# Three dummy matmuls, the first weights on ScalarE's queue, and a first half split one k tile at a time

## The chip, the cores and the metric

The kernel runs on one core of one Trainium2 chip. The metric is device time in microseconds, the median of the runs. Engines are TensorE (PE, with its weight loads as PEld), VectorE (DVE), ScalarE (ACT), GpSimd (POOL) and SyncE (SP). Transfers are issued by SP (queue q1), ScalarE (q10) and GpSimd (q0), and all queues are served by the same 16 DMA engines.

## What is computed

Two layers run one after the other on 256 tokens of width 2048, in float32. The first layer puts 16 meta tokens ahead (272 rows), normalizes, multiplies by a wide input matrix and runs two branches: attention over keys that an indexer selects, and a chunkwise gated recurrence. The second layer has a filter branch computed with Fourier transforms, grouped attention with rotary positions, and a gated feed-forward of width 5632. For the front of the program only this part of the reference matters:

```python
def rms_norm(x, gain):
    y = xf * lax.rsqrt(jnp.mean(xf * xf, axis=-1, keepdims=True) + EPS)
    return (y * gain.astype(jnp.float32)).astype(x.dtype)
...
h = rms_norm(x, norm_g)
proj = h @ w_in          # [272, 2048] @ [2048, 12368]
```

The kernel multiplies x by the gain ahead of the product and applies the reciprocal root to the product's rows, so the front needs the gain vector (norm_g) but not yet the root.

## The kernel before

**Products.** Every float32 product is made from rounded parts: an operand is split into a high part (rounded, written by ScalarE) and a low part (what is left, subtracted by VectorE), and a product is three matmuls, high by high, high by low and low by high (`product`, L2077 to L2080). The weights stream through in units of 512 rows by 512 columns (1 MB), four units to a chunk of 512 output columns. A unit lies in one of four slots of `raw` and is two halves of two k tiles (128 rows each). `split_half` on ScalarE (L758) writes `w_hi` for a half (128 x 1024), `split_half` on VectorE (L1280) writes `w_lo`, and TensorE's `chunk` waits for `split_lo` of the half, then issues its 12 matmuls (two k tiles, two blocks of 128 tokens, three matmuls). `w_hi` and `w_lo` have four slots each.

**Order.** There is no planner. Each engine's program is written out in order, and counting semaphores join them. A half has a number 8 q + h (chunk q, half h), and work beside the products is hung on these numbers (`branch_step`, `step`). In chunk 0 two more k tiles of x are turned behind each half, so that the operand is always four tiles ahead.

**The front, engine by engine.** SP issues the left half of x (two transfers, 512 KB each), then `raw[:, 0, 0:2]` (the first two k tiles of weights, semaphore `raw_first`, L580), `raw[:, 0, 2:4]` (L581), the second unit, the right half of x, two more units and a narrow block of weights. ScalarE issues the identity (64 KB), the gain vector into `stage_a` (8 KB; these two count `first_in`) and the meta tokens (128 KB). GpSimd waits for the left half of x and then issues thirty small constants.

TensorE waits for a cleared tile, runs `warm(4)` (four float32 matmuls on that tile, results unused; each is two passes in the profile), waits for `first_in`, turns the gain vector (L2210), waits until VectorE has copied it to `vec_a` (L1329), turns four k tiles of x (`turn_h`, L2204, which waits for x), runs `warm(2)` and enters chunk 0.

ScalarE evicts each turned tile as `h_hi`, scaled by the gain (`keep_h_hi`, L772), four of them, and then comes to the first `split_half`, which waits for `raw_first`. VectorE follows with `h_lo` (`keep_h_lo`, L1333), four of them, and then its `split_half`. In chunk 0 TensorE waits for `h_lo_kept` of both k tiles and for `split_lo` ahead of each half.

Of the kernel before, what the change touches and what calls it, by code (L numbers as in the profile page):

```python
# [15 lines left out]
F32 = mybir.dt.float32  # L16
F32R = mybir.dt.float32r
I32 = mybir.dt.int32
ALU = mybir.AluOpType
ACT = mybir.ActivationFunctionType  # L20
AX_X = mybir.AxisListType.X

P = 128
# [6 lines left out]
W = 512  # L30
# [32 lines left out]
def hybrid_layers(nc, a, out):  # L63

    ctx = ExitStack()
    with ctx:
# [6 lines left out]
        def place(name, shape, dt=F32):  # L73
            t = at(name, shape, dt, spot[0])
            spot[0] += -(-4 * int(np.prod(shape[1:])) // 32) * 32
            return t


        raw = place("raw", [P, 4, 4, W])
        w_hi = place("w_hi", [P, 4, 2, W], F32R)  # L80
        w_lo = place("w_lo", [P, 4, 2, W], F32R)
# [171 lines left out]
        def sem(name):  # L253
            return ctx.enter_context(nc.semaphore(name))
# [19 lines left out]
        meta_hi_kept = sem("meta_hi_kept")  # L274
        meta_lo_kept = sem("meta_lo_kept")
        raw_first = sem("raw_first")
        warm_ready = sem("warm_ready")
        raw_in = [sem(f"raw_in{s}") for s in range(4)]
        split_hi = sem("split_hi")
        split_lo = sem("split_lo")  # L280
# [16 lines left out]
        h_lo_kept = sem("h_lo_kept")  # L297
# [5 lines left out]
        rot_ready = sem("rot_ready")  # L303
        tables_ready = sem("tables_ready")
        rsq_ready = sem("rsq_ready")
        k_rstd = sem("k_rstd")
        k_scaled = sem("k_scaled")
        qk_turned = sem("qk_turned")
        qk_kept = sem("qk_kept")
# [75 lines left out]
        z_spec = sem("z_spec")  # L385
        y_spec = sem("y_spec")
        yh_prod = sem("yh_prod")
        yh_done = sem("yh_done")
        y_done = sem("y_done")
        y_biased = sem("y_biased")  # L390
        y_scaled = sem("y_scaled")
# [19 lines left out]
        w_in, w_branch, w_out = a["w_in"][0], a["w_branch"][0], a["w_out"][0]  # L411

        CHUNKS = [(C_QI, W, 0), (C_QI + W, W, 0), (C_QA, W, 0), (C_QA + W, W, 0),
                  (C_KA, W, 1), (C_VA, W, 1), (C_ZA, W, 0), (C_ZA + W, W, 0), (C_QB, W, 0), (C_QB + W, W, 0),
                  (C_ZB, W, 0), (C_ZB + W, W, 0), (C_FB, W, 1), (C_FB + W, W, 1), (C_IB, W, 1), (C_IB + W, W, 1)]
# [134 lines left out]
        def tile_rows(w, r0, rows, cols):  # L550
            return w[r0:r0 + rows, cols].rearrange("(k p) n -> p k n", p=P)
# [3 lines left out]
        def _(sp):  # L555
            def load_x(c):
                cols = slice(c * BW, (c + 1) * BW)
                for b in range(NT):
                    sp.dma_start(xt[:, b, cols], a["x"][0][b * P:(b + 1) * P, cols]).then_inc(x_in[c], 16)
# [17 lines left out]

            first_cols = slice(CHUNKS[0][0], CHUNKS[0][0] + W)
            load_x(0)
            sp.dma_start(raw[:, 0, 0:2, :], tile_rows(w_in, 0, 2 * P, first_cols)).then_inc(raw_first, 16)  # L580
            sp.dma_start(raw[:, 0, 2:4, :], tile_rows(w_in, 2 * P, 2 * P, first_cols)).then_inc(raw_in[0], 16)  # L581
            load_unit(0, 1, tile_rows(w_in, W, W, first_cols), first=True)
            load_x(1)
# [57 lines left out]
            for s in range(4):  # L641
                q = Q_DOWN + FKT // 4 - 1
# [93 lines left out]
        @block.scalar  # L736
        def _(act):
            act.dma_start(ident[:, :], a["c_ident"]).then_inc(first_in, 16)
            act.dma_start(stage_a[0:16, :], a["norm_g"].rearrange("o (k p) -> (o k) p", p=P)).then_inc(first_in, 16)
            act.dma_start(xm[:, :], a["meta_tokens"]).then_inc(meta_in, 16)  # L740

# [6 lines left out]

            def split_half(q, h, width=W, first=False):

                if first and h == 0:
                    act.wait_ge(raw_first, 16)
                elif h % 2 == 0 or (first and h == 1):
                    act.wait_ge(raw_in[h // 2], 16 * q + 16)
                if not (first and h < 4):

                    act.wait_ge(half_done, 8 * q + h - 3)
                act.activation(w_hi[:, h % 4, :, 0:width], raw[:, h // 2, 2 * (h % 2):2 * (h % 2) + 2, 0:width],  # L758
                               ACT.Copy).then_inc(split_hi, 1)

            n_roots = [0]

# [7 lines left out]
            def keep_h_hi(k):  # L770
                act.wait_ge(h_turned, k + 1)
                act.activation(h_hi[:, k, META:TM], ps[H_BANK[k]][:, 0:T], ACT.Copy, scale=vec_a[:, k:k + 1]  # L772
                               ).then_inc(h_hi_kept, 1)

            for k in range(4):
                keep_h_hi(k)

            def keep_turned_hi(g):
# [247 lines left out]
            def keep_y_hi(g):  # L1026

                for i, (at_slot, bank) in enumerate(YT):
                    if g == at_slot + 2:
                        act.wait_ge(y_turned, i + 1)  # L1030
                        keep_bank(y_hi[:, i // 4, 2 * (i % 4):2 * (i % 4) + 2, :].rearrange("p k t -> p (k t)"),
                                  bank).then_inc(y_hi_kept, 1)

            for n, (c0, width, m) in enumerate(CHUNKS):
                for h in range(8):
                    split_half(n, h, width, first=(n == 0))
                    if n == 1 and h == 3:
                        act.wait_ge(rs_ready, n_roots[0])
                        keep_chunk(0)
                    if h == 2 and n > 1 and n - 1 not in FM:  # L1040
                        keep_chunk(n - 1)
                    branch_step(8 * n + h)
                    keep_y_hi(8 * n + h)
# [224 lines left out]
        def _(dve):  # L1268
# [8 lines left out]
            def split_half(q, h, width=W):  # L1277

                dve.wait_ge(split_hi, 8 * q + h + 1)
                dve.tensor_tensor(w_lo[:, h % 4, :, 0:width], raw[:, h // 2, 2 * (h % 2):2 * (h % 2) + 2, 0:width],  # L1280
                                  w_hi[:, h % 4, :, 0:width].bitcast(F32), ALU.subtract).then_inc(split_lo, 1)
# [49 lines left out]
            def keep_h_lo(k):  # L1331
                dve.wait_ge(h_hi_kept, k + 1)
                dve.scalar_tensor_tensor(h_lo[:, k, META:TM], ps[H_BANK[k]][:, 0:T], vec_a[:, k:k + 1],  # L1333
                                         h_hi[:, k, META:TM].bitcast(F32), ALU.mult, ALU.subtract).then_inc(h_lo_kept, 1)

            for k in range(4):
                keep_h_lo(k)


# [377 lines left out]
            def keep_y_lo(g):  # L1717

                for i, (at_slot, bank) in enumerate(YT):
                    if g == at_slot + 2:  # L1720
                        dve.wait_ge(y_hi_kept, i + 1)
                        part = slice(2 * (i % 4), 2 * (i % 4) + 2)
                        dve.tensor_tensor(y_lo[:, i // 4, part, :].rearrange("p k t -> p (k t)"), ps[bank][:, :],
                                          y_hi[:, i // 4, part, :].rearrange("p k t -> p (k t)").bitcast(F32),
                                          ALU.subtract).then_inc(y_lo_kept, 1)

            for n, (c0, width, m) in enumerate(CHUNKS):
                for h in range(8):
                    split_half(n, h, width)
                    branch_step(8 * n + h)  # L1730
                    keep_y_lo(8 * n + h)

# [231 lines left out]
            for n in range(Q_OUT2 - Q_PROJ2):  # L1964
                q = Q_PROJ2 + n
# [108 lines left out]
        def _(pe):  # L2074
# [38 lines left out]
            def turned(e, h):  # L2113

                pe.wait_ge(turn_lo, 8 * e + h + 1)
# [5 lines left out]
            def chunk(q, halves, left, dsts, width=W, step=None, new=None, fresh=False):  # L2121

                n = 2 * len(halves)
                for x, h in enumerate(halves):
                    if new is not None:
                        turned(new, h)
                    if fresh:

                        pe.wait_ge(y_lo_kept, max(h + 1, 2))
                    if isinstance(q, int) and q == 0:  # L2130
                        pe.wait_ge(h_lo_kept, 2 * h + 2)
                    pe.wait_ge(split_lo, 8 * q + h + 1)
                    for e in range(2):
                        k = 2 * x + e
                        for i, dst in enumerate(dsts):
                            ins = product(dst, left(k, i), w_hi[:, h % 4, e, 0:width], w_lo[:, h % 4, e, 0:width],
                                          k == 0, k == n - 1)
                    ins.then_inc(half_done, 1)
                    if step is not None:
                        step(8 * q + h)  # L2140
                    if isinstance(q, int):
                        turn_step(8 * q + h)
# [50 lines left out]
            def warm(n):  # L2193
                for _ in range(n):
                    pe.matmul(ps[0][:, :], junk[:, 0:P], junk[:, 0:W], start=True, stop=True)
# [9 lines left out]
                ins.then_inc(h_turned, 1)  # L2205

            pe.wait_ge(warm_ready, 1)
            warm(4)
            pe.wait_ge(first_in, 16 * N_FIRST)
            pe.transpose(ps[2][:, 0:KT], stage_a[0:KT, :], ident[0:KT, 0:KT]).then_inc(vec_turned, 1)  # L2210
            pe.wait_ge(vec_kept, 1)
            for k in range(4):
                turn_h(k)
            warm(2)


            def attention_step(g):
# [433 lines left out]
            for n in range(Q_OUT2 - Q_PROJ2):  # L2651
                q = Q_PROJ2 + n
# [174 lines left out]
```

## Time and profile before

| | us |
|---|---|
| median of 3 runs | 2265.32 |
| lowest, highest | 2264.97, 2265.67 |
| profiled execution | 2267.46 |
| its span | 2265.8 |
| TensorE busy | 2243.4 (99%) |
| VectorE busy | 1330.9 (59%) |
| ScalarE busy | 1007.8 (44%) |
| GpSimd busy | 361.0 (16%) |

The profile is one execution. Its span runs from the first instruction to the last, and the time of the execution holds 1.7 us more around it. Busy shares are averages over stages; matmuls overlap in the profile, so the start of one to the start of the next is its cost, and its duration is longer. A column "idle before <- releaser" names what ended an engine's standing still. The granted clock (PEclk) is TensorE's as a share of 2.4 GHz; records of it begin at 5.7 us, and a stretch ahead of that is printed as 1.00.

### The profile page before, as it was taken

To read this page: it belongs to the slowest core of one execution; us is meant where nothing else is said; L and a number is where in the kernel's file an instruction comes from. 1 tells how busy PE (TensorE), PEld (TensorE's weight loads), DVE (VectorE), ACT (ScalarE), POOL (GpSimd) and SP (SyncE) were. 2 spreads that over 40 slices of the span, in tenths; PEclk is the share of its full clock that TensorE was granted. 3 is DMA by queue.
4 is the path that set the end of the run, shared out by engine and by line. 5 is a ranking of instruction groups with operands and counts; after the bars stand their busy time and mean duration, and the time that the engine had idled before them with its cause. 6 is when DMAs were issued, how large, how long until landed. Compare 5 with 4: busy or idle time off the path is not lost.

```text
span 2265.8 us, 27795 instructions
## 1 busy us (share of the span) xinstructions
PE 2243.4 (99%) x10668; PEld 1830.2 (81%) x10668; DVE 1330.9 (59%) x1727; ACT 1007.8 (44%) x1347; POOL 361.0 (16%) x456
## 2 busy tenths in 40 slices
PE   9999999999999999999999999999999999999999
PEld 7787779988878777788777888888888888878887
DVE  5977556968575554756566555554544454444454
ACT  6445544243444435555433344445444444444443
POOL 4878788810000000000000000000000000000000
PEclk9999999999999999999999999999999999999999
DMA  8555646344456644554525655555555555555553
GB/s 270 178 170 159 188 155 193 123 154 162 148 191 206 220 146 133 179 171 147 178 98 172 212 185 180 187 184 186 185 186 185 185 185 185 185 183 188 185 185 130
DMA packets 196225, 398.97 MB, mean 176 GB/s; under 512 B 9704, under 2 KB 35571, under 8 KB 190609
## 3 DMA queue, kind: packets, MB, share of 16 engines
q1 hardware_dynamic: 191216, 386.56, 51.5%
q0 software_dynamic: 2848, 7.66, 1.3%
q10 hardware_dynamic: 2064, 3.42, 0.5%
q8 instruction: 67, 1.10, 0.2%
q14 instruction: 30, 0.24, 0.0%
HBM read 395.51 MB, written 2.10 MB: 175 GB/s over the span
## 4 chain that ended last, share of the span: by engine, by line
PE 91%; DVE 6%; ACT 2%; issue 1%; ACTq 0%; DVEq 0%
PE ps L2078 26%; PE ps L2080 26%; PE ps L2079 26%; DVE w_lo L1280 2%; PE ps L2161 2%; PE ps L2162 2%; PE ps L2163 2%; PE ps L2344 1%; PE ps L2109 1%; PE ps L2642 1%; PE ps L2628 1%; PE ps L2500 1%; ACT sqj L861 1%; ACT w_hi L758 0%; PE ps L2688 0%
## 5 line engine op out<-in xcount | busy, mean ns | idle before, releaser
L1280 DVE TENSOR_TENSOR w_lo<-raw,w_hi 128x1024 fp32r<-128x1024 f32 x720 | 889.9, 1246 | 702.4 <-ACT w_hi L758 698.0
L758 ACT ACTIVATE w_hi<-raw 128x1024 fp32r<-128x1024 f32 x720 | 751.2, 1057 | 676.9 <-PE ps L2080 627.2
L2078 PE MATMUL ps<-w_hi,h_hi 128*128 128x512 f32 x1408 | 568.7, 404 | 6.9 <-DVE w_lo L1280 6.8
L2080 PE MATMUL ps<-w_hi,h_lo 128*128 128x512 f32 x1408 | 556.4, 395 | 0.0
L2079 PE MATMUL ps<-w_lo,h_hi 128*128 128x512 f32 x1408 | 554.5, 394 | 0.0
L2078 PEld LDWEIGHTS ps<-w_hi,h_hi 128*128 128x128 f32 x1408 | 266.1, 189 | 70.7 <-issue 9.0
L2080 PEld LDWEIGHTS ps<-w_hi,h_lo 128*128 128x128 f32 x1408 | 265.4, 188 | 62.1
L2079 PEld LDWEIGHTS ps<-w_lo,h_hi 128*128 128x128 f32 x1408 | 265.9, 189 | 58.7 <-issue 1.4
L2078 PE MATMUL ps<-w_hi,x1t 128*128 128x512 f32 x672 | 272.5, 405 | 5.2 <-DVE w_lo L1280 5.2
L2079 PE MATMUL ps<-w_lo,x1t 128*128 128x512 f32 x672 | 266.6, 397 | 0.0
L2080 PE MATMUL ps<-w_hi,x1t 128*128 128x512 f32 x672 | 266.1, 396 | 0.0
L2078 PEld LDWEIGHTS ps<-w_hi,x1t 128*128 128x128 f32 x672 | 126.6, 188 | 38.1 <-DVE w_lo L1280 6.8
L2080 PEld LDWEIGHTS ps<-w_hi,x1t 128*128 128x128 f32 x672 | 126.6, 188 | 30.5
L2079 PEld LDWEIGHTS ps<-w_lo,x1t 128*128 128x128 f32 x672 | 126.6, 188 | 29.3 <-issue 1.0
L2078 PE MATMUL ps<-w_hi,st_hi 128*128 128x512 f32 x352 | 140.5, 399 | 0.7 <-ACT hid L1213 0.7
L2080 PE MATMUL ps<-w_hi,st_lo 128*128 128x512 f32 x352 | 138.7, 394 | 0.0
L2079 PE MATMUL ps<-w_lo,st_hi 128*128 128x512 f32 x352 | 138.0, 392 | 0.0
L2161 PE MATMUL ps<-h_hi,w_hi 128*128 128x272 f32 x384 | 112.1, 292 | 1.9 <-DVE w_lo L1280 1.9
L2162 PE MATMUL ps<-h_lo,w_hi 128*128 128x272 f32 x384 | 110.9, 289 | 0.0
L2163 PE MATMUL ps<-h_hi,w_lo 128*128 128x272 f32 x384 | 110.7, 288 | 0.0
L2080 PEld LDWEIGHTS ps<-w_hi,st_lo 128*128 128x128 f32 x352 | 66.1, 188 | 17.0
L2078 PEld LDWEIGHTS ps<-w_hi,st_hi 128*128 128x128 f32 x352 | 66.1, 188 | 16.2 <-ACT hid L1213 1.0
(454 smaller groups left out, 2328.8 us busy)
## 6 DMA issues: line engine op xcount, KB each, us to landing
raw<-w_in SPq DMA_DIRECT2D x163, 1024.0 KB, 5.3
raw<-w_ffn_gate SPq DMA_DIRECT2D x44, 1024.0 KB, 5.2
raw<-w_ffn_up SPq DMA_DIRECT2D x44, 1024.0 KB, 5.2
raw<-w_ffn_down SPq DMA_DIRECT2D x44, 1024.0 KB, 4.8
raw<-w_out SPq DMA_DIRECT2D x32, 1024.0 KB, 5.1
raw<-w_branch SPq DMA_DIRECT2D x16, 1024.0 KB, 5.0
raw<-w_br_hyena SPq DMA_DIRECT2D x8, 1024.0 KB, 5.0
raw<-w_br_attn SPq DMA_DIRECT2D x8, 1024.0 KB, 5.0
```

What stands on the lines that cost most here:

```text
L758: act.activation(w_hi[:, h % 4, :, 0:width], raw[:, h // 2, 2 * (h % 2):2 * (h % 2) + 2, 0:width], ACT.Copy).then_inc(split_hi, 1)
L861: ins = act.activation(sqj[0:p, :], src, ACT.Square, accum_out=ms[0:p, col:col + 1])
L1280: dve.tensor_tensor(w_lo[:, h % 4, :, 0:width], raw[:, h // 2, 2 * (h % 2):2 * (h % 2) + 2, 0:width], w_hi[:, h % 4, :, 0:width].bitcast(F ...
L2078: pe.matmul(dst, hi, w_h, start=first, stop=False)
L2079: pe.matmul(dst, hi, w_l, start=False, stop=False)
L2080: return pe.matmul(dst, lo, w_h, start=False, stop=last)
L2109: ins = pe.transpose(ps[bank][:, x * T + b * P:x * T + (b + 1) * P], src[:, b, c:c + P], ident[:, :])
L2161: pe.matmul(dst, w_h, h_hi[:, k, :], start=(k == 0), stop=False)
L2162: pe.matmul(dst, w_h, h_lo[:, k, :], start=False, stop=False)
L2163: ins = pe.matmul(dst, w_l, h_hi[:, k, :], start=False, stop=(k == KT - 1))
L2344: ins = pe.matmul(ps[6 + c][:, i * (P // 2):(i + 1) * (P // 2)].rearrange("p (k n) -> p k n", n=2 ** (lev - 1)), kl[:, i, cols], half_bloc ...
L2500: ins = pe.matmul(ps[SPEC_BANK[i % 3]][:, :], left, right, start=(b == 0), stop=(b == NT - 1))
```

## The change

ScalarE's queue gets the first two k tiles of weights as its second transfer, ahead of the gain vector and the meta tokens, and SP no longer issues them. TensorE runs three dummy matmuls at the start and none after the turns of x. ScalarE and VectorE treat the first half apart: two evictions, then the half in two pieces of one k tile each (`split_first`), then the other two evictions. Two new semaphores (`first_hi`, `first_lo`) count the first piece, and two unused ones are gone. In the first half TensorE waits for each k tile's `h_lo` and `w_lo` by itself.

```diff
--- before.py
+++ after.py
@@ -274,6 +274,8 @@
         meta_hi_kept = sem("meta_hi_kept")
         meta_lo_kept = sem("meta_lo_kept")
         raw_first = sem("raw_first")
+        first_hi = sem("first_hi")
+        first_lo = sem("first_lo")
         warm_ready = sem("warm_ready")
         raw_in = [sem(f"raw_in{s}") for s in range(4)]
         split_hi = sem("split_hi")
@@ -577,7 +577,6 @@
 
             first_cols = slice(CHUNKS[0][0], CHUNKS[0][0] + W)
             load_x(0)
-            sp.dma_start(raw[:, 0, 0:2, :], tile_rows(w_in, 0, 2 * P, first_cols)).then_inc(raw_first, 16)
             sp.dma_start(raw[:, 0, 2:4, :], tile_rows(w_in, 2 * P, 2 * P, first_cols)).then_inc(raw_in[0], 16)
             load_unit(0, 1, tile_rows(w_in, W, W, first_cols), first=True)
             load_x(1)
@@ -736,6 +735,8 @@
         @block.scalar
         def _(act):
             act.dma_start(ident[:, :], a["c_ident"]).then_inc(first_in, 16)
+            act.dma_start(raw[:, 0, 0:2, :], tile_rows(w_in, 0, 2 * P, slice(CHUNKS[0][0], CHUNKS[0][0] + W))
+                          ).then_inc(raw_first, 16)
             act.dma_start(stage_a[0:16, :], a["norm_g"].rearrange("o (k p) -> (o k) p", p=P)).then_inc(first_in, 16)
             act.dma_start(xm[:, :], a["meta_tokens"]).then_inc(meta_in, 16)
 
@@ -748,15 +749,19 @@
 
             def split_half(q, h, width=W, first=False):
 
-                if first and h == 0:
-                    act.wait_ge(raw_first, 16)
-                elif h % 2 == 0 or (first and h == 1):
+                if h % 2 == 0 or (first and h == 1):
                     act.wait_ge(raw_in[h // 2], 16 * q + 16)
                 if not (first and h < 4):
 
                     act.wait_ge(half_done, 8 * q + h - 3)
                 act.activation(w_hi[:, h % 4, :, 0:width], raw[:, h // 2, 2 * (h % 2):2 * (h % 2) + 2, 0:width],
                                ACT.Copy).then_inc(split_hi, 1)
+
+            def split_first():
+
+                act.wait_ge(raw_first, 16)
+                act.activation(w_hi[:, 0, 0, :], raw[:, 0, 0, :], ACT.Copy).then_inc(first_hi, 1)
+                act.activation(w_hi[:, 0, 1, :], raw[:, 0, 1, :], ACT.Copy).then_inc(split_hi, 1)
 
             n_roots = [0]
 
@@ -772,7 +777,10 @@
                 act.activation(h_hi[:, k, META:TM], ps[H_BANK[k]][:, 0:T], ACT.Copy, scale=vec_a[:, k:k + 1]
                                ).then_inc(h_hi_kept, 1)
 
-            for k in range(4):
+            for k in range(2):
+                keep_h_hi(k)
+            split_first()
+            for k in range(2, 4):
                 keep_h_hi(k)
 
             def keep_turned_hi(g):
@@ -1033,7 +1041,8 @@
 
             for n, (c0, width, m) in enumerate(CHUNKS):
                 for h in range(8):
-                    split_half(n, h, width, first=(n == 0))
+                    if n or h:
+                        split_half(n, h, width, first=(n == 0))
                     if n == 1 and h == 3:
                         act.wait_ge(rs_ready, n_roots[0])
                         keep_chunk(0)
@@ -1333,7 +1342,19 @@
                 dve.scalar_tensor_tensor(h_lo[:, k, META:TM], ps[H_BANK[k]][:, 0:T], vec_a[:, k:k + 1],
                                          h_hi[:, k, META:TM].bitcast(F32), ALU.mult, ALU.subtract).then_inc(h_lo_kept, 1)
 
-            for k in range(4):
+            def split_first():
+
+                dve.wait_ge(first_hi, 1)
+                dve.tensor_tensor(w_lo[:, 0, 0, :], raw[:, 0, 0, :], w_hi[:, 0, 0, :].bitcast(F32),
+                                  ALU.subtract).then_inc(first_lo, 1)
+                dve.wait_ge(split_hi, 1)
+                dve.tensor_tensor(w_lo[:, 0, 1, :], raw[:, 0, 1, :], w_hi[:, 0, 1, :].bitcast(F32),
+                                  ALU.subtract).then_inc(split_lo, 1)
+
+            for k in range(2):
+                keep_h_lo(k)
+            split_first()
+            for k in range(2, 4):
                 keep_h_lo(k)
 
 
@@ -1726,7 +1747,8 @@
 
             for n, (c0, width, m) in enumerate(CHUNKS):
                 for h in range(8):
-                    split_half(n, h, width)
+                    if n or h:
+                        split_half(n, h, width)
                     branch_step(8 * n + h)
                     keep_y_lo(8 * n + h)
 
@@ -2127,11 +2149,16 @@
                     if fresh:
 
                         pe.wait_ge(y_lo_kept, max(h + 1, 2))
-                    if isinstance(q, int) and q == 0:
+                    first_step = isinstance(q, int) and q == 0 and h == 0
+                    if isinstance(q, int) and q == 0 and h:
                         pe.wait_ge(h_lo_kept, 2 * h + 2)
-                    pe.wait_ge(split_lo, 8 * q + h + 1)
+                    if not first_step:
+                        pe.wait_ge(split_lo, 8 * q + h + 1)
                     for e in range(2):
                         k = 2 * x + e
+                        if first_step:
+                            pe.wait_ge(h_lo_kept, e + 1)
+                            pe.wait_ge((first_lo, split_lo)[e], 1)
                         for i, dst in enumerate(dsts):
                             ins = product(dst, left(k, i), w_hi[:, h % 4, e, 0:width], w_lo[:, h % 4, e, 0:width],
                                           k == 0, k == n - 1)
@@ -2205,13 +2232,12 @@
                 ins.then_inc(h_turned, 1)
 
             pe.wait_ge(warm_ready, 1)
-            warm(4)
+            warm(3)
             pe.wait_ge(first_in, 16 * N_FIRST)
             pe.transpose(ps[2][:, 0:KT], stage_a[0:KT, :], ident[0:KT, 0:KT]).then_inc(vec_turned, 1)
             pe.wait_ge(vec_kept, 1)
             for k in range(4):
                 turn_h(k)
-            warm(2)
 
 
             def attention_step(g):
```

## Rows read from the trace of the kernel before

**Rows 1.** The page, busy time by engine: us (share of the span) xinstructions.
```profile
PE 2243.4 (99%) x10668; PEld 1830.2 (81%) x10668; DVE 1330.9 (59%) x1727; ACT 1007.8 (44%) x1347; POOL 361.0 (16%) x456
```

**Rows 2.** The page, chain that ended last, by engine.
```profile
PE 91%; DVE 6%; ACT 2%; issue 1%; ACTq 0%; DVEq 0%
```

**Rows 3.** Waits of TensorE, whole span: us in total, times, longest us.
```profile
PE ps L2078 <- DVE w_lo L1280: 13.3, 12, 2.8
```

**Rows 4.** Timeline of TensorE, 0 to 13 us: start, us, what, idle before.
```profile
1.59 5.73 PE L2195 MATMUL ps<-junk 128*128 128x512 f32 x8 [1.59 <-DVE junk L1324]
...
5.17 1.30 PE L2195 MATMUL ps<-junk 128*128 128x512 f32 x2
...
7.25 0.23 PE L2210 MATMUL ps<-ident,stage_a 16*128 16x16 f32 x1
7.75 1.09 PE L2204 MATMUL ps<-ident,xt 128*128 128x128 f32 x8 [0.27 <-DVE vec_a L1329]
...
12.14 0.47 PE L2078 MATMUL ps<-w_hi,h_hi 128*128 128x512 f32 x1 [1.58 <-DVE w_lo L1280]
```

**Rows 5.** Timeline of ScalarE and VectorE, 8 to 13 us.
```profile
8.23 1.57 ACT L772 ACTIVATE h_hi<-ps,vec_a 128x256 fp32r<-128x256 f32 x4 [4.66 <-PE ps L2204]
...
9.67 2.08 ACT L758 ACTIVATE w_hi<-raw 128x1024 fp32r<-128x1024 f32 x2
...
10.78 2.36 DVE L1280 TENSOR_TENSOR w_lo<-raw,w_hi 128x1024 fp32r<-128x1024 f32 x2 [0.30 <-ACT w_hi L758]
```

**Rows 6.** Windows: stretch, its us, busy us of each engine, PEclk, DMA share, GB/s.
```profile
12.10:60.00 47.90, 47.86 (x253) 40.04 (x254) 30.87 (x55) 30.87 (x41) 21.56 (x38) 1.00 0.83 270
```

**Rows 7.** DMA issues, 1.30 to 1.36 and 1.75 to 1.80: KB, us to landing.
```profile
xt<-x SPq DMA_DIRECT2D x1, 512.0 KB, 5.5
...
stage_a<-norm_g ACTq DMA_DIRECT2D x1, 8.0 KB, 4.5
...
raw<-w_in SPq DMA_DIRECT2D x1, 512.0 KB, 7.5
```

**Rows 8.** DMA packets: 2.0-4.5 (two rows), 4.5-5.5, 0-8.5, 0-9.0, 6.5-8.0.
```profile
q1 hardware_dynamic: 137, 0.53, 76.2%
q10 hardware_dynamic: 118, 0.06, 8.0%
...
q1 hardware_dynamic: 109, 0.41, 100.8%
...
DMA packets 771, 1.80 MB, mean 212 GB/s; under 512 B 89, under 2 KB 233, under 8 KB 755
...
DMA packets 873, 1.99 MB, mean 221 GB/s; under 512 B 97, under 2 KB 241, under 8 KB 857
...
DMA packets 111, 0.21 MB, mean 142 GB/s; under 512 B 10, under 2 KB 10, under 8 KB 110
```

**Rows 9.** Groups by form, 0 to 40 us: busy us, mean ns, idle.
```profile
L1642 DVE TENSOR_TENSOR kw_lo<-kw_raw,kw_hi 128x1280 fp32r<-128x1280 f32 x1 | 1.5, 1492 | 0.7 <-ACT kw_hi L992 0.7
...
L992 ACT ACTIVATE kw_hi<-kw_raw 128x1280 fp32r<-128x1280 f32 x1 | 1.3, 1272 | 0.0
```

**Rows 10.** Timeline of TensorE at 207, and windows of low clock.
```profile
206.97 0.64 PE L2078 MATMUL ps<-w_hi,h_hi 128*128 128x512 f32 x1 [2.83 <-DVE w_lo L1280]
...
207.00:210.50 3.50, 3.50 (x9) 2.72 (x10) 3.36 (x8) 0.00 (x0) 3.27 (x4) 0.51 0.16 21
...
831.00:835.00 4.00, 4.00 (x11) 3.13 (x11) 1.30 (x2) 0.00 (x0) 0.00 (x0) 0.50 0.29 81
1142.40:1145.70 3.30, 3.30 (x9) 2.48 (x8) 1.14 (x2) 0.00 (x0) 0.00 (x0) 0.50 0.58 173
```

**Rows 11.** Timeline of all engines, 20 to 26 us.
```profile
20.79 1.06 ACT L758 ACTIVATE w_hi<-raw 128x1024 fp32r<-128x1024 f32 x1 [1.32 <-DMA raw<-w_in]
...
21.88 1.23 DVE L1280 TENSOR_TENSOR w_lo<-raw,w_hi 128x1024 fp32r<-128x1024 f32 x1 [1.87 <-ACT w_hi L758]
...
25.00 0.48 PE L2078 MATMUL ps<-w_hi,h_hi 128*128 128x512 f32 x1
```

More of the change, by code:

```diff
@@ L305, in hybrid_layers @@
         rsq_ready = sem("rsq_ready")
-        k_rstd = sem("k_rstd")
         k_scaled = sem("k_scaled")
@@ L387, in hybrid_layers @@
         yh_prod = sem("yh_prod")
-        yh_done = sem("yh_done")
         y_done = sem("y_done")
```

## The prediction

> **What bounds the kernel now.** I read the shares of the engines first. TensorE is busy for 2243.4 of 2265.8 us and no other engine comes near it [rows 1]. The chain of work that ended last says the same: 91% of it is TensorE, 6% VectorE, 2% ScalarE [rows 2]. So a change at the front can give only what TensorE stands still there, and a microsecond added there reaches the end unless something later absorbs it. The list of TensorE's waits shows how little there is: 13.3 us in 12 waits for a split of weights, the longest 2.8 us [rows 3].
>
> The front is then read in order of time. Eight dummy passes (four matmuls of two passes each) run from 1.59, the norm vector is turned at 7.25, four k tiles of x from 7.75 to about 8.7, four more dummy passes follow, and the first product of projection 1 starts at 12.14, after 1.58 us of standing still, so from 10.56 [rows 4]. That first product is what the change wants earlier. Before it stand ScalarE's four evictions (8.23 to 9.80), its rounding of the first two halves from 9.67, and VectorE's remainder from 10.78, the first of which ends at about 12.01 [rows 5]. Behind it TensorE is busy for all but 0.04 us up to 60 [rows 6], so every step of its start would be kept, until a transfer is late.
>
> **The change, part by part.**
>
> *Dummies.* Two passes fewer ahead: the fifth and sixth end at 5.17 + 1.30 = 6.47 [rows 4], where eight end at 7.32. That frees 0.85 us, if what comes next has landed. In the kernel before it had: the norm vector and the second half-block of x are issued about 1.3; the one lands 4.5 us later, at 5.8, the other 5.5 later, at 6.8 [rows 7]. On their own, fewer dummies would start the turns at about 6.85 and not at 7.75. The two later dummies (four passes up to 10.56) lie in a gap and cost nothing to remove as work; as activity they are priced below.
>
> *The weights on ScalarE's queue.* The transfer (512 KB) was third on SP, issued about 1.8, landed 7.5 later at 9.3 [rows 7]. It is now second on ScalarE's queue, where the norm vector stood, so issued about 1.3. The two issues behind it on ScalarE come one issue later, which ScalarE, idle up to 8.23 [rows 5], has to spare; SP's come one earlier. But the norm vector and the meta tokens are pushed behind it, on the same queue. I read the order of packets: from 2.0 to 4.5 us, q1 (x) started 137 packets and q10 (the identity) 118, that is one and one, while one kind is 4 KB and the other 0.5 KB [rows 8]. So q10's packets get every second turn, and what was issued behind 256 packets of weights waits for all of them.
>
> When do these end? The identity's 128 packets are done near 4.9. By then x has some 180 of its 256 packets (137 by 4.5, 109 more in the next microsecond [rows 8]), so 75 of the weights' packets alternate with the rest of x and 181 with as many 2 KB packets of SP's next load. The sum is 1.05 (x) + 0.07 (identity) + 0.52 (weights) + 0.37 = 2.01 MB. The queues had moved 1.80 MB by 8.5 us and 1.99 by 9.0, which is 380 GB/s [rows 8]; in the kernel before, the same weights (1.05 + 0.52 + 0.20 = 1.77 MB) had their last packet at about 8.4 and landed at 9.3, a lag of 0.9. So at that pace the weights and the norm vector land at 9.95. The lower side: between 6.5 and 8.0 the transfers ran at 142 GB/s, against those 380 after it [rows 8]; if that slow stretch is gone, (380 - 142) x 1.5 us = 0.35 MB or 0.95 us come off, 9.0; if ScalarE's weights also don't share with SP's next load, 0.37 MB or 1.0 us more, 8.0. I take 9.5, in the upper half, since nothing says that the slow stretch goes. x lands later too, by 75 packets of 2 KB at 380 GB/s: 0.4 us, 7.2, hidden behind the norm vector.
>
> The Trainium skill says this as a rule (DMA: Bandwidth & Descriptors, "Queues, rings and completion order"): an engine takes turns between queue rows packet by packet and works through one row in its order. The trace's 137 against 118 agrees. It speaks against this change: a small vector which the whole front needs is queued behind half a megabyte. The same page ("Issuing engines are not separate DMA queues") holds that a second issuing engine saves only issue time; here that would be the 0.5 us between the two issues of rows 7.
>
> *From the norm vector to the first product.* With the distances of before: turn of the vector to turns of x 0.5 (7.25 to 7.75), to the first eviction 0.48 (8.23), two evictions 0.72 (four take 8.23 to 9.67 when work follows), the rounding of one k tile, the remainder of one k tile, and the gaps around (0.05 ahead of the turn, 0.05 ahead of the remainder, 0.13 to the product) [rows 4, 5]. One k tile of 512 columns has no row; 1024 columns take 1.06 us on ScalarE and 1280 take 1.27, so 0.83 ns a column and 0.63 us; VectorE 1.23 and 1.49, about 1.05 a column, 0.68 us [rows 9, 11]. From below both could be half (0.53, 0.61), from above whole (1.06, 1.22); I take the slope. Sum: 0.05 + 0.5 + 0.48 + 0.72 + 0.63 + 0.05 + 0.68 + 0.13 = 3.24. First product at 9.5 + 3.24 = 12.74, which is **+0.6 us** (from 8.0: 11.24, -0.9; from 9.95: 13.2, +1.1).
>
> *The finer waits.* The second k tile's remainder ends 0.68 after the first's, and the first tile's six products last 6 x 0.23 = 1.4: hidden. ScalarE then does evictions 3 and 4 (0.72) and the next half (1.06), VectorE its remainder: ready 3.4 us after the first product at most with the two roundings overlapped, against 2.8 of products and 0.44 of turns. About 0.1 may show; counted at zero, since at the lower clock below the products take longer. One more instruction on each of two engines, 0.2 us, is hidden by their waits.
>
> *TensorE's activity.* Before, dummies and turns kept it working from 1.59 to 10.56, and it stood 1.58 us at full clock. Now it has nothing from 6.47 to 9.5, then 0.3 and 1.1 us of turns, then nothing to 12.74. Rows on both sides: after standing 2.83 us the product at 206.97 took 0.64 us, the granted clock was 0.51 from 207.0 to 210.5 (the 1.2 GHz level, half of 2.4), and only 9 products began in those 3.5 us; it was 0.50 again from 1142.4 to 1145.7, behind another wait for a split [rows 10], while after the 1.58 us before 12.14 it stayed at 1.00 [rows 4, 6]. Six microseconds with 1.4 of small turns in them are far nearer to the first two. The price by those rows: 3.3 to 3.5 us at half speed hold the work of half of it, so **+1.7 us**. Bounds: 0, if it isn't lowered; twice, 3.4, if the low stretch covers waiting and work and isn't left at once.
>
> **Sum:** +0.6 + 1.7 = +2.3 us. The profiled execution took 2267.46 (span 2265.8 and 1.7 around it), which gives 2269.8 for it. The median of the runs is 2265.32, 2.1 below the profiled one, and to that I apply the same +2.3: **2267.6**.
>
> **Rivals.**
>
> *A. The norm vector isn't held up.* The landing follows issue time and not the order on q10: vector at 6.3, x at 7.2, turns at 7.2, two evictions by 8.4, weights landed by 8.4, first product near 9.9, more than 2 us ahead of 12.14. Not all is kept: the loads behind are transfer-bound. The half that ScalarE could take up only at 20.79, when its weights landed, gets its remainder from 21.88 to 23.11 and is used from 25.00 [rows 11], so at most 25.00 - 23.11 = 1.9 us survive: 2263.4. For it: the vector is 8 KB, and x, issued at the same time as it, has not been held up by ScalarE's queue so far. Against: the turns of packets [rows 8].
>
> *B. The clock holds.* Only +0.6: 2265.9. For it: 1.58 us idle cost nothing. Against: the stand is twice as long.
>
> *C. A later low stretch goes.* The clock fell around 207 and 1142 behind a wait each [rows 10]. When such a wait comes 2 us later, it may fall elsewhere or not at all (-1.7), net +0.6: 2265.9; both, 2264.2. The other way is open less: 12 waits sum to 13.3 us with a longest of 2.8 [rows 3], so most are near 1 us, less than the 1.58 that cost nothing.
>
> *D. Slower by more.* The late vector (9.95) with a low clock that lasts two stretches, as one did that took all of 831 to 835 at 0.50 [rows 10]: +1.1 + 3.4 + 0.3 for the turns at half speed = +4.8: 2270.1. It decides where the vector lands behind 9.9 and the clock is already low when the turns begin. For it: such a long stretch exists. Against: it needs both at once.
>
> **How the numbers follow.** Forecast 0.42, A 0.18, B 0.12, C 0.20, D 0.08. About 0.2%, 4.5 us, is what can be told from no change: below 2260.8 or above 2269.8. Faster than that needs A and both stretches of C, 0.03; slower is D, 0.08; the same 0.89. The range goes from A (2263.4) to just below D, 2269.8.
>
> **What would show it.** Norm vector landing 7.5 to 8.5 us after an issue at 1.8, the turn of it at 9.0 to 10.0 and not 6.5; meta tokens right behind; the first product at 11.3 to 13.2; products 0.43 apart for 3 to 4 us there. A turn of the vector before 7.5 would make the step of the queue wrong; products 0.23 apart from the first would make the clock's term wrong; a wait on a weight transfer at the fifth half would show A. ScalarE's 512-column rounding at 0.63 and VectorE's at 0.68 check the slope.

## The result and the profile after

The changed kernel takes 2270.34 us (median of 10 runs, 2268.01 to 2273.17) against 2265.49 (10 runs, 2264.02 to 2268.62): 4.85 us more, a ratio of 1.0020 with a 95% interval of 1.0011 to 1.0028. A second reading later gave 2273.43 (6 runs) against 2266.32, 1.0032 (1.0020 to 1.0044). The forecast was 2267.6 with a range to 2269.8: the change costs more, and in the first reading about what rival D said (2270.1). The profiled execution took 2270.79, its span 2269.1.

The timeline of TensorE in the changed kernel (start, us, what, idle before):

```profile
1.59 4.80 PE L2222 MATMUL ps<-junk 128*128 128x512 f32 x6 [1.59 <-DVE junk L1333]
10.22 0.28 PE L2237 MATMUL ps<-ident,stage_a 16*128 16x16 f32 x1 [3.83 <-DMA stage_a<-norm_g]
10.77 1.97 PE L2231 MATMUL ps<-ident,xt 128*128 128x128 f32 x8 [0.27 <-DVE vec_a L1338]
13.78 0.76 PE L2100 MATMUL ps<-w_hi,h_hi 128*128 128x512 f32 x1 [1.05 <-DVE w_lo L1348]
14.34 0.63 PE L2101 MATMUL ps<-w_lo,h_hi 128*128 128x512 f32 x1
14.77 0.63 PE L2102 MATMUL ps<-w_hi,h_lo 128*128 128x512 f32 x1
...
18.61 0.63 PE L2102 MATMUL ps<-w_hi,h_lo 128*128 128x512 f32 x1
19.04 0.69 PE L2231 MATMUL ps<-ident,xt 128*128 128x128 f32 x4
19.48 0.48 PE L2100 MATMUL ps<-w_hi,h_hi 128*128 128x512 f32 x1
19.80 0.39 PE L2101 MATMUL ps<-w_lo,h_hi 128*128 128x512 f32 x1
```

The second row is the answer to the row at 7.25 of [rows 4]: TensorE stands 3.83 us, and what it waits for is the transfer of the gain vector. The turns of x start at 10.77 and not at 7.75, the first product at 13.78 and not at 12.14. Its successors come 0.43 apart, up to the turns at 19.04, where the kernel before had 0.23. The transfers of the changed kernel, issued at 1.34 and 1.82 on ScalarE's queue (KB, us to landing), answer to [rows 7]:

```profile
raw<-w_in ACTq DMA_DIRECT2D x1, 512.0 KB, 8.5
...
stage_a<-norm_g ACTq DMA_DIRECT2D x1, 8.0 KB, 8.4
```

So the vector lands near 10.2 (5.8 before), right behind the weights in front of it, and the weights near 9.9, which is 0.6 us later than on SP's queue (9.3). The load that should come earlier came later. Packets of the changed kernel from 6.5 to 8.0, from 8.3 to 10.0 and from 0 to 9.0:

```profile
DMA packets 323, 0.63 MB, mean 419 GB/s; under 512 B 22, under 2 KB 30, under 8 KB 319
...
DMA packets 158, 0.28 MB, mean 164 GB/s; under 512 B 32, under 2 KB 35, under 8 KB 154
q10 hardware_dynamic: 27, 0.04, 14.0%
...
DMA packets 1010, 2.26 MB, mean 251 GB/s; under 512 B 94, under 2 KB 238, under 8 KB 997
```

The slow stretch of [rows 8] (142 GB/s from 6.5 to 8.0) isn't gone. It comes later, and now 27 packets of ScalarE's queue lie in it, with the landings of the weights and of the vector in it or right behind it (9.9 and 10.2). The bytes were as predicted: by 8.0 us 2.02 MB had moved, 1.41 MB of it on SP's queue and 0.61 on ScalarE's, where the prediction had 2.01 in all. It is the landing that took longer, about 2 us behind that mark in place of 0.9.

The windows of the changed kernel (stretch, its us, busy us of PE, PEld, DVE, ACT, POOL, granted clock, DMA share, GB/s):

```profile
9.00:13.70 4.70, 2.25 (x9) 1.75 (x9) 1.80 (x5) 2.21 (x6) 4.70 (x9) 0.50 1.03 314
13.70:19.20 5.50, 5.42 (x13) 4.18 (x14) 3.68 (x5) 2.35 (x4) 5.50 (x11) 0.50 1.05 348
19.20:40.00 20.80, 20.80 (x115) 17.05 (x114) 12.63 (x18) 15.17 (x23) 4.41 (x10) 1.00 0.99 319
207.00:210.50 3.50, 3.21 (x14) 2.36 (x13) 3.43 (x5) 2.29 (x4) 3.34 (x3) 1.00 0.63 239
418.60:425.40 6.80, 6.80 (x33) 6.80 (x32) 6.66 (x10) 0.00 (x0) 6.22 (x8) 0.50 0.25 64
835.00:838.40 3.40, 3.40 (x10) 2.66 (x9) 1.09 (x1) 0.00 (x0) 0.00 (x0) 0.50 0.29 69
```

The clock is at its lower level from 9.0 to 19.2, three times as long as the stretch that the forecast had priced. The later ones of [rows 10] change places: the one at 207 is gone, one of 6.8 us is new at 418.6. That can't be put down to the change, since they differ between two profiles of one kernel too. In the second profile of the change the front is the same (low for 10.2 us), but the clock is low near 146 for 3.4 us and not at 418. The finer split alone (e5 and e10 below) has low stretches of 3.4 us near 828 and 1138 in one profile, with a span of 2262.5 us, and only the one at 828 in the other, with 2260.1.

**The front as a sum.** The turns behind half 0 are a good mark, since everything of the first half is ahead of them: 15.01 before, 19.04 after, 4.03 us later. Of these, 1.64 are the first product's start and 2.39 the half itself (5.26 us in place of 2.87, at the lower clock). The rest to the medians' 4.85 isn't seen in the two profiles, whose spans differ by only 3.3 us (2269.1 and 2265.8, each with its own later low stretches). It lies in what differs between the executions.

### The profile page after: what moved, and what is told of

Its sections match the earlier page's. It is cut to its first block, busy times and chain, and to the rows that moved or that the text cites. A ratio compares the mean times of both kernels' runs of the same rounds, so it can differ in the third digit from the quotient of the medians.

```text
span 2269.1 us, 27786 instructions
## 1 busy us (share of the span) xinstructions
PE 2244.0 (99%) x10662; PEld 1832.1 (81%) x10662; DVE 1333.8 (59%) x1728; ACT 1007.8 (44%) x1348; POOL 356.7 (16%) x456
## 4 chain that ended last, share of the span: by engine, by line
PE 91%; DVE 5%; ACT 2%; issue 1%; DMA 0%; ACTq 0%; DVEq 0%
PE ps L2100 26%; PE ps L2102 26%; PE ps L2101 26%; PE ps L2188 2%; PE ps L2189 2%; PE ps L2190 2%; DVE w_lo L1289 2%; PE ps L2370 1%; PE ps L2131 1%; PE ps L2668 1%; PE ps L2654 1%; PE ps L2526 1%; ACT sqj L869 1%; ACT w_hi L757 0%; PE ps L2714 0%
```

## The experiments

Each kernel was timed against the kernel before on the same chip. In the table, "mark" is the start of the first four turns behind half 0 in its profile (15.01 before), the difference is that of the medians, and the clock is the mean of the granted clock over its timed runs (0.9974 to 0.9976 for the kernel before on the same chips).

| kernel | first product | mark | median, difference | ratio, 95% | clock |
|---|---|---|---|---|---|
| the change (profile after) | 13.78 | 19.04 | 2270.34, +4.9 | 1.0020 (1.0011 to 1.0028) | 0.9950 |
| the change again (e12) | 13.91 | 19.16 | 2273.43, +7.1 | 1.0032 (1.0020 to 1.0044) | 0.9942 |
| queue alone (e2) | 15.13 | 18.00 | 2268.96, +3.3 | 1.0014 (1.0004 to 1.0023) | 0.9974 |
| dummies alone (e3) | 11.62 | 16.04 | 2268.50, +2.8 | 1.0013 (1.0004 to 1.0022) | 0.9960 |
| split alone (e5) | 10.64 | 13.51 | 2264.74, -1.5 | 0.9994 (0.9985 to 1.0003) | 0.9978 |
| split alone again (e10) | 10.64 | 13.51 | 2265.64, -0.5 | 0.9997 (0.9988 to 1.0006) | 0.9976 |
| change, no queue move (e6) | 10.62 | 14.99 | 2267.32, +1.1 | 1.0002 (0.9993 to 1.0011) | 0.9965 |
| change, vector first (e1) | 11.73 | 16.15 | 2268.69, +3.0 | 1.0012 (1.0003 to 1.0021) | 0.9960 |
| change, covered (e4) | 13.46 | 16.33 | 2266.49, +0.8 | 1.0004 (0.9995 to 1.0013) | 0.9976 |
| vector first, dummies back (e7) | 12.02 | 14.88 | 2265.23, -1.0 | 0.9996 (0.9987 to 1.0006) | 0.9977 |
| split, tile loads (e8) | 10.40 | 13.27 | 2265.13, -1.1 | 0.9996 (0.9987 to 1.0005) | 0.9976 |
| the same, 3 + 2 dummies (e9) | 10.33 | 13.20 | 2264.01, -2.2 | 0.9991 (0.9982 to 1.0000) | 0.9981 |
| that again (e11) | 10.18 | 13.04 | 2264.97, -1.4 | 0.9991 (0.9982 to 1.0000) | 0.9978 |

Marks and medians don't move alike. In the five readings without dummies behind the turns (the change twice, dummies alone, vector first, no queue move) the median is worse than the mark says by 0.8 to 3.0 us, and the mean clock is lower (0.9942 to 0.9965). In the eight with them it lies between 0.9 us below and 1.0 above (0.9974 to 0.9981). So the kernels without these dummies lose more on average than their profiles show; whether in the front or later isn't shown, since executions other than the profiled one leave only their mean clock.

**The two issues exchanged** (e1), on the changed kernel:

```diff
-            act.dma_start(raw[:, 0, 0:2, :], ...).then_inc(raw_first, 16)
             act.dma_start(stage_a[0:16, :], a["norm_g"]...).then_inc(first_in, 16)
+            act.dma_start(raw[:, 0, 0:2, :], ...).then_inc(raw_first, 16)
```

> The changed kernel with two issues of ScalarE's queue exchanged: the gain vector goes ahead of the 512 KB of weights, all else as changed. Queue theory (the vector is late because it stands behind the weights on one queue, and the long stand lowers the clock): the vector lands before 6.5 us, not at 10.2, the turns of x start when x lands, near 7.2, the weights land near 9.5, so the first product starts near 11, at full clock, and the median is 2263 to 2266. Rival, the finer split with its extra waits costs the time: the front stays slow, 2268 to 2271. Rival, the dummies that are gone cost it by themselves: the vector is early but the products still run 0.43 us apart for some us, 2266 to 2268.

The turns start at 6.73, 4 us earlier than in the changed kernel, so the order on the queue is what held the vector. But the median is only 1.9 us better (+3.0 and not +4.9; against the second reading of the change, +7.1, it is 4.1), over what the queue theory had. The vector's transfer and that of the weights (e1, issued at 1.34 and near 1.8), and TensorE:

```profile
stage_a<-norm_g ACTq DMA_DIRECT2D x1, 8.0 KB, 4.8
...
raw<-w_in ACTq DMA_DIRECT2D x1, 512.0 KB, 8.4
```

```profile
6.73 1.09 PE L2231 MATMUL ps<-ident,xt 128*128 128x128 f32 x8 [0.27 <-DVE vec_a L1338]
11.73 0.47 PE L2100 MATMUL ps<-w_hi,h_hi 128*128 128x512 f32 x1 [3.91 <-DVE w_lo L1348]
```

Now the weights are the last to arrive, near 10.2, and TensorE stands 3.91 us for them, and the clock falls behind it: it is low from 12.2 for 3.4 us, and the mark is at 16.15. The rival of the dummies fits (vector early, products slow at first, a little over its 2266 to 2268). The time alone would also fit the rival of the finer split (2268 to 2271); e5 rules that one out.

**The queue alone** (e2), on the kernel before:

```diff
-            sp.dma_start(raw[:, 0, 0:2, :], tile_rows(w_in, 0, 2 * P, first_cols)).then_inc(raw_first, 16)
...
+            act.dma_start(raw[:, 0, 0:2, :], ...).then_inc(raw_first, 16)
             act.dma_start(stage_a[0:16, :], a["norm_g"]...).then_inc(first_in, 16)
```

> The kernel before with one edit: the first 512 KB of weights go out second on ScalarE's queue, ahead of the gain vector, in place of SP's. Four and two dummies, no finer split. Queue theory: the vector lands near 10.2, the turns start near 10.7, first product near 14 to 14.5 us (12.14 before); the stand from 7.3 to 10.2 is 2.9 us, so the clock may be lowered for one stretch and is back earlier than in the changed kernel: 2267.5 to 2270. Theory of the split or of the dummies: the front is at most 0.5 us later, 2265 to 2266.5.

TensorE of that kernel:

```profile
10.24 0.23 PE L2211 MATMUL ps<-ident,stage_a 16*128 16x16 f32 x1 [2.77 <-DMA stage_a<-norm_g]
10.74 1.09 PE L2205 MATMUL ps<-ident,xt 128*128 128x128 f32 x8 [0.27 <-DVE vec_a L1330]
11.66 1.88 PE L2196 MATMUL ps<-junk 128*128 128x512 f32 x4
15.13 0.47 PE L2079 MATMUL ps<-w_hi,h_hi 128*128 128x512 f32 x1 [1.58 <-DVE w_lo L1281]
18.00 0.60 PE L2205 MATMUL ps<-ident,xt 128*128 128x128 f32 x4
```

Its window from 13 to 20 us (columns as above):

```profile
13.00:20.00 7.00, 5.42 (x25) 4.05 (x24) 4.83 (x7) 4.20 (x6) 7.00 (x13) 1.00 1.05 350
```

From the turns to the first product it takes 15.13 - 10.74 = 4.39, exactly as before (12.14 - 7.75), so the whole front is moved by 2.99 us, and the medians differ by 3.3. That is over my 14 to 14.5 for the product. The clock held through a stand of 2.77 us in this profile, and over the runs it is that of the kernel before (0.9974). So the queue costs 3 us as pure lateness. In the whole change 1.6 of it are seen at the product, since the split takes back the rest.

**The dummies alone** (e3), on the kernel before: `warm(4)` to `warm(3)`, and `warm(2)` behind the turns taken out.

> The kernel before with one edit: three dummy matmuls ahead and none after the turns. Queue theory: the vector lands at 5.8 and x at 6.8 as before, so the turns start about 0.8 us earlier; ScalarE then waits for the weights at 9.3 (before it began on them at 9.67), so the first product gains 0.3 us at most. TensorE stands from about 8 to 11.8, 3.8 us: the clock is lowered for one stretch or two. 2265 to 2269, by the clock alone. Dummies theory: all of the change's loss is here, 2269 to 2271.

The first product comes at 11.62, 0.5 us earlier, and the kernel is slower by 2.8 us. Two windows of it (columns as above):

```profile
11.60:16.00 4.40, 4.38 (x12) 3.43 (x13) 2.43 (x2) 1.06 (x1) 4.40 (x8) 0.61 1.05 369
16.00:20.00 4.00, 4.00 (x23) 3.35 (x22) 2.10 (x3) 2.12 (x4) 4.00 (x9) 1.00 1.07 334
```

12 matmuls begin in the first 4.4 us and 23 in the next 4.0. This is the clock alone: it fell near 12.4, behind a stand of 3.74 us, and stayed low for 3.4 us, and the mark is 1.0 us late although the product was 0.5 early. The profiled run lost least of all its runs; the median lost 1.8 us more than its mark, and the mean clock is 0.9960.

**The change with TensorE kept at work** (e4): `warm(3)` to `warm(7)`, and `warm(2)` put back behind the turns.

> The changed kernel with the late vector kept, but TensorE kept at work: seven dummy matmuls ahead (to about 9.8 us) and two after the turns. Queue theory: the vector still lands near 10.2, the first product near 13.3 us, but at full clock, products 0.23 us apart: what is left is the late start alone, 1 to 1.5 us over the kernel before, 2266 to 2267.5. If it stays at 2269 to 2271, the clock in the front isn't what the loss is made of; if it falls to 2265 or less, the late start costs nothing and the clock is all of it.

```profile
1.59 8.69 PE L2222 MATMUL ps<-junk 128*128 128x512 f32 x14 [1.59 <-DVE junk L1333]
10.27 0.23 PE L2237 MATMUL ps<-ident,stage_a 16*128 16x16 f32 x1
10.76 1.09 PE L2231 MATMUL ps<-ident,xt 128*128 128x128 f32 x8 [0.27 <-DVE vec_a L1338]
...
13.46 0.47 PE L2100 MATMUL ps<-w_hi,h_hi 128*128 128x512 f32 x1
```

The vector is as late, but nothing is idle: the product comes at 13.46, the mark at 16.33, 1.3 us after that of before and 2.7 before that of the change. The median falls by about 4 us against the changed kernel, to +0.8. So of the change's loss (first reading) about 1 is lateness that is left after the split's gain, and 3 to 4 are the clock.

**The finer split alone** (e5), on the kernel before: the functions `split_first` and the waits of TensorE's first step as in the change, the queue and the dummies as before.

> The kernel before with the finer split of the first half alone; the weights stay third on SP's queue, four and two dummies stay. Both theories agree that the turns start at 7.75 and the weights land at 9.3. Queue theory: ScalarE rounds the first k tile (0.62 us) from about 9.35, VectorE's remainder (0.69) is ready near 10.7, and the first product starts near 10.9 at full clock, where the kernel before has 12.14: 1.2 us gained, 2264 to 2265. Split theory (more waits and instructions cost time): 2266 or more.

ScalarE, VectorE and TensorE of that kernel:

```profile
9.13 0.63 ACT L762 ACTIVATE w_hi<-raw 128x512 fp32r<-128x512 f32 x1
...
9.80 0.69 DVE L1347 TENSOR_TENSOR w_lo<-raw,w_hi 128x512 fp32r<-128x512 f32 x1
...
10.64 0.47 PE L2099 MATMUL ps<-w_hi,h_hi 128*128 128x512 f32 x1
```

The pieces take 0.63 and 0.69 us, as the slope had said, and the product comes at 10.64, right behind the second dummies. The mark is 1.5 us early. The medians are 1.5 and, once more, 0.5 us below before, each with an interval that reaches 1: the sign is likely, not shown by the times alone.

> The finer split alone once more, beside the two others on the same chip: the first product near 10.9 and 1.0 to 1.5 us below the kernel before, if the first reading was no chance.

The second profile of it has the product at 10.64 and the mark at 13.51 again; the median is 0.5 us below before, less than the 1.0 to 1.5 expected.

**The change without the move of the queue** (e6): the load back on SP, all else as changed.

> The changed kernel with one part undone: the weights are back third on SP's queue, so the gain vector is second on ScalarE's. Finer split, three dummies ahead and none later, as changed. Queue theory: the vector lands at 5.8, x at 6.8, weights at 9.3, first product near 10.9, but TensorE has stood 3 us since the turns, so the products run 0.43 us apart for one stretch or so (1.7 us lost against 1.2 gained): 2265 to 2268, like the run with the dummies alone less 1. If the queue isn't the cause it stays at 2269 to 2271.

TensorE of that kernel, and its window of low clock:

```profile
10.62 0.47 PE L2099 MATMUL ps<-w_hi,h_hi 128*128 128x512 f32 x1 [2.79 <-DVE w_lo L1347]
...
11.70:15.10 3.40, 3.40 (x10) 2.51 (x9) 1.86 (x3) 1.30 (x2) 3.40 (x7) 0.50 1.06 379
```

The product is at 10.62 as with the split alone, but TensorE stood 2.79 us for it, and the clock was low from 11.7 for 3.4 us: the mark is at 14.99, no gain left. The stand is as long as that of e2 (2.77), where the clock held. What lay ahead of it differs, 5.88 us of dummies there and 1.06 us of turns here, so the length of a stand alone doesn't say what the clock will do. This kernel is 3.8 us below the change (+1.1 against +4.9), which is the queue's part once more.

**The exchanged issues with the dummies back** (e7): as e1, with `warm(4)` and `warm(2)`.

> The changed kernel with the vector ahead of the weights on ScalarE's queue, and with four and two dummies again. The weights land at 10.2 there, as in the run that exchanged the two without the dummies, so the first product is at about 11.7 with full clock, 0.4 us ahead of the kernel before: 2264.5 to 2266.5, against 2268.7 for the same queue without the dummies. If the dummies don't matter, it stays near 2268.7.

Against e1 the dummies are worth 4.0 us at the medians (+3.0 and -1.0), though the product is 0.3 later (12.02). The clock held (0.9977).

**One transfer per k tile** (e8), and with three dummies ahead (e9), on the split alone:

```diff
-            sp.dma_start(raw[:, 0, 0:2, :], tile_rows(w_in, 0, 2 * P, first_cols)).then_inc(raw_first, 16)
+            for e, landed in enumerate((raw_first, raw_second)):
+                sp.dma_start(raw[:, 0, e, :], w_in[e * P:(e + 1) * P, first_cols]).then_inc(landed, 16)
...
                 act.activation(w_hi[:, 0, 0, :], raw[:, 0, 0, :], ACT.Copy).then_inc(first_hi, 1)
+                act.wait_ge(raw_second, 16)
```

> The split alone on the kernel before, and the first 512 KB of weights go out on SP's queue as two transfers of one k tile, each with its own semaphore. The first k tile should land some 0.7 us ahead of the pair, near 8.5, so that ScalarE's rounding can start right behind its second eviction, at 8.95 in place of 9.35, and the first product comes near 10.6 us, where the second dummies end: 0.2 to 0.4 us less than the split alone, 2264.3 to 2265. If the transfers behind then set the pace, or the first k tile doesn't land ahead of the second, it equals the split alone.

> The same with three dummies ahead in place of four, two later ones kept. The turns start when x has landed, near 6.85 in place of 7.75, the evictions are done by 8.3, and ScalarE waits for the first k tile, near 8.5: first product near 10.1. The dummies end at 9.7, so TensorE stands 0.4 us only and the clock holds: 2263.5 to 2264.7. If the clock is lowered all the same, 2265 to 2267.

> The best version so far once more (finer split, one transfer per k tile on SP's queue, three dummies ahead and two later), beside the changed kernel on the same chip: first product near 10.3 us, 1.5 to 2.2 us below the kernel before if the first reading was no chance, and at 1.0000 if it was.

The first k tile lands at 8.7 to 8.9, only 0.2 to 0.6 us ahead of the pair, and the product comes at 10.40 with four dummies ahead, at 10.33 and 10.18 with three. With three dummies ahead TensorE stood at most 0.23 us before the product, the products came 0.23 us apart from the first, so nothing was lost to the clock there, and this version has the lowest times of the study: 2264.01 and 2264.97, both times a ratio of 0.9991 with an interval from 0.9982 to 1.0000. Against the kernel before that is 1.4 to 2.2 us at the edge of what can be told; against the changed kernel, timed on the same chip beside the second reading, it is 8.5 us.

> The changed kernel once more, unaltered: the vector near 10.2 us, the first product near 13.8, the first turns behind half 0 4 us later than before. If the front explains the loss, the difference is 4.0 us or little more, with part of it from where low stretches fall later; a second reading near 4.9 would say that about 1 us comes on top of the front in the mean of the runs.

This second reading of the change was +7.1, above both of my figures, while its profile shows the same front (vector 8.5 us behind its issue, product 13.91, mark 19.16). The runs of the change spread with their clock: 2274.5 on average at a granted clock of 0.993 (2 runs), 2273.2 at 0.994 (4), 2270.5 at 0.995 (7), 2269.1 at 0.996 (3). The kernel before does it too, 2265.6 at 0.998 (58 runs) and 2272.1 at 0.995 (2). So what differs between runs goes with how long TensorE is kept at the lower level. The two profiles of the change differ only behind the front, in the later low stretches named above.

## Why the prediction was wrong, step by step

**What bounds the kernel:** right. A front that is late is late at the end; e2's 2.99 us at the mark came out as 3.3.

**The queue:** the mechanism was right and decided the sign. The Trainium skill's rule (DMA: Bandwidth & Descriptors, "Queues, rings and completion order") that one row is worked through in its order is borne out by e1 and the change: the same 8 KB land 4.8 us after their issue ahead of the weights and 8.4 behind them. How many packets are taken in one turn the counts don't show (137 and 118 over 16 engines), and the sum didn't need it. The size was off: "I take 9.5", below my own upper bound of 9.95, because I left room for the slow stretch to go. It moved instead, and the landing was 10.2, outside both bounds. The bytes of the sum were right (2.02 MB by 8.0 us); the lag of 0.9 us from there to the landing was the wrong term, with about 2 us measured. Rival A, the vector not held up, is refuted by that landing.

**From the vector to the first product:** 3.24 forecast, 13.78 - 10.2 = 3.6 measured. The pieces of one k tile were exact (0.62 and 0.69). What was missing is that turns and evictions ran behind a clock already low: first turn to first eviction 0.72 us (11.49 - 10.77) and not 0.48, which is most of the difference. Product +1.6 in place of +0.6.

**The clock, the step that failed most:** "3.3 to 3.5 us at half speed hold the work of half of it, so +1.7". One stretch was priced, and it was taken to begin where the products begin. The clock was low before the turns (9.0) and up to 19.2, and the first half alone lost 2.39 us. e3 shows the same term by itself, e4 the change without it. The sum at the mark is +1.64 + 2.39 = +4.0, where I had +2.3. Of the 1.7 between them, 0.7 is the landing, 0.3 the path to the product and 0.7 the half itself, so about 1.0 goes to the clock, if the path is counted with it.

The front alone would have left the time inside the range (2265.3 + 4.0 = 2269.4). What took it beyond 2269.8 is the 0.8 us by which the medians differ from the marks, 3.0 in the second reading, and for that the prediction had no term. That D's number (2270.1) was met so closely is partly luck: D had +1.1 for the vector and +3.4 and +0.3 for the clock, all in the front, where +4.0 was measured.

**The chances:** D asked for a late vector and a long low clock, and I gave it 0.08 because "it needs both at once". With the dummies gone they aren't independent: each tenth of a us by which the vector is later is added to the stand. A low clock came in all five readings without them, whether the vector was late or not, and the long one (10.2 us) in both of the change, where it was late. So once the vector was thought late, D deserved far more, and the range should have gone beyond 2270; how much more is a judgement. B (the clock holds) did occur, but in e2, where the dummies stayed. C was half right: the stretch at 207 went, and another came at 418.6, but such stretches come and go between profiles of one kernel, so as a gain it can't be counted.

**Costed at nothing and right:** the extra instructions and waits of the split. Its gain I had counted only inside the sum of 3.24 and never by itself: it is 1.5 us at the mark when alone (13.51 against 15.01) and 1.7 behind the late vector (16.33 in e4, 18.00 in e2). With the queue and the dummies left alone it is kept at the mark; in the medians it is 1.5 and 0.5, within their intervals.

**Whether the parts add up:** queue +3.0, dummies +1.0, split -1.5 at their marks give +2.5 against the change's +4.0. The remaining 1.5 is what the parts cost together beyond their sum: e2 has the late vector and no low stretch in the front, e3 the missing work and one of 3.4 us, and only both give a stand of 3.83 us, small turns and another stand of 1.05, with a clock that is low for 10.2 us. The medians' parts (+3.3, +2.8 and -1.5, or -0.5 by the second reading) give +4.6 to +5.6 against +4.9 and +7.1, so there the extra cost isn't clear of the scatter.

## What to carry to other kernels

A small transfer that the first step needs goes ahead of every big one on its queue; moving a big load to a second queue does not make it early, since both queues draw on the same engines (159 packets of one and 164 of the other from 6.5 to 8.0 us in the changed kernel), and it can hold up what stands behind it. Dummy work ahead of a matmul stream is not idle fat: before taking it out, or before making anything land later, add up how long TensorE stands, and don't take it that a low clock begins with the products and lasts one stretch. In the changed kernel it fell at 9.0, 2.6 us into the stand, and stayed low for 10.2 us; in e1, e3 and e6 it fell 0.5 to 1.0 us behind the first product and stayed low for 3.4. Two conditions with a common cause don't get the small chance of two independent ones.

## What was not expected of the hardware

The 142 GB/s stretch of the start of the kernel before isn't tied to a time: with the weights on another queue it moved from 6.5-8.0 to 8.3-10.0 (164 GB/s), and its cause is open. A single k tile of 256 KB, issued ahead of its neighbour, landed only 0.2 to 0.6 us before the pair of 512 KB did (8.7 to 8.9 against 9.1 to 9.3). And with the same kernel the profile's front hardly moves (product 13.78 and 13.91), while the times of its runs spread from 2268.0 to 2274.8, in step with the mean granted clock. Stands of the same length, 2.77 and 2.79 us, left the clock at its upper level in e2 and lowered it in e6.
